# A two-layer hybrid decoder trunk: the memory's norm factors behind the memory rows, the first weight block in two halves, the sine's steps one block later

## What is computed

```python
def rms_norm(x, g):
    xf = x.astype(F32)
    y = xf * lax.rsqrt(jnp.mean(xf * xf, axis=-1, keepdims=True) + EPS)
    return (y * g.astype(F32)).astype(x.dtype)
...
    inv = 1.0 / (ROPE_BASE ** jnp.linspace(0.0, 1.0, half, dtype=F32))
    ang = positions.astype(F32)[..., None] * inv
    cos = jnp.cos(ang)[:, :, None, :]
    sin = jnp.sin(ang)[:, :, None, :]
...
    for l in range(DEPTH):
        g = norm_g[l]
        h = rms_norm(x, g[0])
        z = h @ w_in[l]
        ...
        x = x + rms_norm(mix @ w_out[l], g[1])
        mem_n = rms_norm(mem, g[6])
        x = x + rms_norm(memory_attention(rms_norm(x, g[2]), mem_n, x_wq[l], x_wkv[l], x_wo[l]), g[3])
        h = rms_norm(x, g[4])
        f = jnp.square(jax.nn.relu(h @ w_up[l])) @ w_down[l]
        x = x + rms_norm(f, g[5])
    return x
```

## Time and profile before

| | |
|---|---|
| median of 3 runs | 1506.36 us (1506.22 to 1506.47) |
| the profiled execution | 1506.58 us, of which the profile's span is 1504.5 us |
| PE busy | 1483.1 us, 99% of the span |
| DVE busy | 882.4 us, 59% |
| ACT busy | 634.4 us, 42% |
| POOL busy | 380.3 us, 25% |
| DMA | 162.09 MB, mean 108 GB/s; 288 GB/s in the first fortieth of the span |
| the chain that ended last | PE 94%, DVE 2%, DMA 1%, ACT 1%, issue 1% |

### The profile page before, as it was taken

The page is one execution under the profiler, slowest core; times in us unless marked ns, Lnnn a source line. Parts: engine busy times, 40 slices in busy tenths (PEclk is TensorE's granted clock), DMA queues, the critical chain, the costliest instruction groups (busy, mean ns, idle before and its releaser), DMA issues.

```text
span 1504.5 us, 19092 instructions
## 1 busy us (share of the span) xinstructions
PE 1483.1 (99%) x7842; PEld 1267.1 (84%) x7842; DVE 882.4 (59%) x1010; ACT 634.4 (42%) x883; POOL 380.3 (25%) x272
## 2 busy tenths in 40 slices
PE   8999999999999999999999999999999999999997
PEld 7878898888898888888898888988888988888886
DVE  5345556724367666575982465756245585756658
ACT  6335424524344343443562454335344352434344
POOL 2001720300053422315030028102001715151422
PEclk9999999999999999999999999999999999999999
DMA  8333131431223424152343232135203342433402
GB/s 288 90 98 101 53 112 65 150 122 54 94 106 115 137 85 162 62 168 99 112 133 119 64 95 86 67 105 175 84 29 112 112 147 79 141 110 112 140 28 98
DMA packets 83237, 162.09 MB, mean 108 GB/s; under 512 B 3664, under 2 KB 19792, under 8 KB 83152
## 3 DMA queue, kind: packets, MB, share of 16 engines
q1 hardware_dynamic: 81712, 158.35, 31.5%
q10 hardware_dynamic: 1440, 2.53, 0.5%
HBM read 158.78 MB, written 2.10 MB: 107 GB/s over the span
## 4 chain that ended last, share of the span: by engine, by line
PE 94%; DVE 2%; DMA 1%; ACT 1%; issue 1%; POOL 0%; SPq 0%; POOLq 0%; DVEq 0%; ACTq 0%
PE proj L688 26%; PE proj L690 25%; PE proj L689 25%; PE work L888 2%; PE work L690 2%; PE work L688 2%; PE work L689 2%; PE work L717 2%; PE work L867 2%; PE work L753 1%; DMA w_raw<-in_x_wkv_dram 1%; PE work L764 1%; PE work L743 1%; PE work L842 1%; PE work L821 0%
## 5 line engine op out<-in xcount | busy, mean ns | idle before, releaser
L1379 DVE TENSOR_TENSOR w_lo<-w_raw,w_hi 128x2048 fp32r<-128x2048 f32 (+1 forms) x103 | 234.8, 2280 | 274.9 <-ACT w_hi L1078 274.6
L688 PE MATMUL proj<-hT_hi,w_hi 128*128 128x512 f32 (+1 forms) x800 | 298.5, 373 | 0.0
L689 PE MATMUL proj<-hT_lo,w_hi 128*128 128x512 f32 (+1 forms) x800 | 297.7, 372 | 0.0
L690 PE MATMUL proj<-hT_hi,w_lo 128*128 128x512 f32 (+1 forms) x800 | 297.7, 372 | 0.0
L1078 ACT ACTIVATE w_hi<-w_raw 128x2048 fp32r<-128x2048 f32 (+1 forms) x103 | 185.3, 1799 | 234.2 <-PE proj L690 232.2
L688 PE MATMUL proj<-w_hi,hT_hi 128*128 128x512 f32 (+1 forms) x640 | 238.5, 373 | 3.5 <-ACT kmT L1182 2.2
L690 PE MATMUL proj<-w_hi,hT_lo 128*128 128x512 f32 (+1 forms) x640 | 232.3, 363 | 0.0
L689 PE MATMUL proj<-w_lo,hT_hi 128*128 128x512 f32 (+1 forms) x640 | 231.8, 362 | 0.0
L690 PEld LDWEIGHTS proj<-hT_hi,w_lo 128*128 128x128 f32 x800 | 150.7, 188 | 26.3
L689 PEld LDWEIGHTS proj<-hT_lo,w_hi 128*128 128x128 f32 x800 | 150.7, 188 | 26.1
L688 PEld LDWEIGHTS proj<-hT_hi,w_hi 128*128 128x128 f32 x800 | 150.7, 188 | 26.0
(11 more groups left out here) (197 smaller groups left out, 2446.3 us busy)
## 6 DMA issues: line engine op xcount, KB each, us to landing
w_raw<-in_w_up_dram SPq DMA_DIRECT2D x32, 1024.0 KB, 5.7
w_more<-in_w_down_dram SPq DMA_DIRECT2D x24, 1024.0 KB, 5.1
w_raw<-in_w_in_dram SPq DMA_DIRECT2D x28, 768.0 KB, 4.4
w_raw<-in_x_wkv_dram SPq DMA_DIRECT2D x15, 1024.0 KB, 5.1
w_raw<-in_w_out_dram SPq DMA_DIRECT2D x8, 1024.0 KB, 5.0
w_raw<-in_x_wq_dram SPq DMA_DIRECT2D x8, 1024.0 KB, 5.1
w_raw<-in_x_wo_dram SPq DMA_DIRECT2D x8, 1024.0 KB, 5.1
w_hs<-in_w_down_dram SPq DMA_DIRECT2D x8, 1024.0 KB, 5.1
```

The lines of the kernel that those rows point to most:

```text
L688: nc.tensor.matmul(dst, l_hi, r_hi, start=first, stop=False, skip_group_check=more)
L689: nc.tensor.matmul(dst, l_hi, r_lo, start=False, stop=False, skip_group_check=more)
L690: return nc.tensor.matmul(dst, l_lo, r_hi, start=False, stop=last, skip_group_check=more)
L1379: nc.vector.tensor_tensor(w_lo[:, slot, :, 0:cols], w_raw[:, raw, :, 0:cols], w_hi[:, slot, :, 0:cols].bitcast(F32), ALU.subtract).then_in ...
```

## The change

The memory's norm factors are issued by SP behind the two memory tiles, and no longer by ACT ahead of everything. ACT and DVE serve the first memory tile's turned rows ahead of block 0's first half, and the second tile's ahead of the second half. PE has a function of its own for block 0 (`first_block`): for all four tiles it multiplies the first half (two of the four 128-row parts), then for all four the second. The first half waits for three of the four turned lo parts and for a new semaphore on the first half's w_lo. DVE makes w_lo of block 1 ahead of the angle's steps. ACT's sin, cos and Exp-table steps move from ahead of the loop into block 1, behind w_hi of block 2.

```diff
             for t in range(MT):
                 sp.dma_start(mems[:, t], mem[0, t * P:(t + 1) * P]).then_inc(mem_first[t], 16)
+            load_gain(0, "mem")
             for h in range(2):
...
+            def first_block():
+
+                for h in range(2):
+                    if h:
+                        pe.wait_ge(w_lo_done, nth(w_lo_done, 0, 1))
+                    else:
+                        pe.wait_ge(turned_lo, nth(turned_lo, 0, -1))
+                        pe.wait_ge(w_first_lo, 1)
+                    for t in range(4):
+                        r = slice(t * P, (t + 1) * P)
+                        if h == 0:
+                            pe.wait_ge(added, nth(added, 0, t + 1 - T))
+                        for k in (2 * h, 2 * h + 1):
+                            mm = three_passes(proj[:, t, 0:MEM], w_hi[:, 0, k, r], w_lo[:, 0, k, r],
+                                              memT_hi[:, k], memT_lo[:, k], k == 0, False)
+                        if h:
+                            mm.then_inc(tile_done, 1)
+                pe.wait_ge(turned_lo, nth(turned_lo, 0, 0))
...
-                    if name == "km0":
+                    if name == "km0" and l == 0:
+                        first_block()
+                    elif name == "km0":
...
             start_counts(act, emptied, p_copied, c_copied, x_exped, x_copied)
-            act.dma_start(gains[:, GAIN_SLOT["mem"]], norm_g[0:1, GAIN["mem"]].broadcast_to([P, D])).then_inc(gain_loaded["mem"], 16)
             act.dma_start(ident[:], c_ident).then_inc(ident_loaded, 16)
...
-            for t in range(MT):
-                turn_hi(PROLOGUE, ("memk", t), memT_hi, t)
+
+            turn_hi(PROLOGUE, ("memk", 0), memT_hi, 0)
+            first_hi(0)
+            turn_hi(PROLOGUE, ("memk", 1), memT_hi, 1)
+            first_hi(1)
             split_hi(PROLOGUE, BLOCKS + 1)
...
-            act.wait_ge(trig_done, 1)
-            nc.scalar.activation(sin[:], angle[:], ACT.Sin)
-            nc.scalar.activation(cos[:], turns[:], ACT.Sin).then_inc(trig_done, 1)
-            nc.scalar.activation(table[:], minus_half[:, 0:1], ACT.Exp)
+
+            def turn_positions():
+                act.wait_ge(trig_done, 1)
+                nc.scalar.activation(sin[:], angle[:], ACT.Sin)
+                nc.scalar.activation(cos[:], turns[:], ACT.Sin).then_inc(trig_done, 1)
+                nc.scalar.activation(table[:], minus_half[:, 0:1], ACT.Exp)
...
                     if 0 < b < HEAD_BLOCKS - 1:
                         head_split(l, b + 1)
+                    if (l, b) == (0, 1):
+                        turn_positions()
                     before_block(l, b)
...
-            for t in range(MT):
-                turn_lo(PROLOGUE, ("memk", t), memT_hi, memT_lo, t)
+            turn_lo(PROLOGUE, ("memk", 0), memT_hi, memT_lo, 0)
+            first_lo(0)
+            turn_lo(PROLOGUE, ("memk", 1), memT_hi, memT_lo, 1)
+            first_lo(1)
+            split_lo(PROLOGUE, BLOCKS + 1)
             setup_steps = [0]
...
             dve.sem_inc(trig_done, 1)
-
-            split_lo(PROLOGUE, BLOCKS + 1)
```

More of the change, by code:

```diff
@@ L438, in trunk @@
         w_first_hi = ctx.enter_context(nc.semaphore("w_first_hi"))
+        w_first_lo = ctx.enter_context(nc.semaphore("w_first_lo"))
         const_loaded = ctx.enter_context(nc.semaphore("const_loaded"))
@@ L1031, in _ @@
                         b = FIRST_BLOCK[name] + kb
+                        if l == 0 and b == 0:
+                            continue
                         if t < tiles:
@@ L1327, in _, with first_hi @@
                 nc.scalar.activation(squares[:, t], mems[:, t], ACT.Square, accum_out=mem_sumsq[:, t:t + 1]).then_inc(mem_summed, 1)
-            for h in range(2):
+            def first_hi(h):
                 k = slice(BK // 2 * h, BK // 2 * (h + 1))
@@ L1815, in _, with first_lo @@
                 norm_mem(PROLOGUE, "memk", t)
-            for h in range(2):
+            def first_lo(h):
                 k = slice(BK // 2 * h, BK // 2 * (h + 1))
@@ L1821, in _ @@
                     dve.wait_ge(w_first_hi, 1)
-                part_lo = nc.vector.tensor_tensor(w_lo[:, 0, k], w_raw[:, 0, k], w_hi[:, 0, k].bitcast(F32), ALU.subtract)
-                if h:
-                    part_lo.then_inc(w_lo_done, 1)
-            for t in range(MT):
-                turn_lo(PROLOGUE, ("memk", t), memT_hi, memT_lo, t)
+                nc.vector.tensor_tensor(w_lo[:, 0, k], w_raw[:, 0, k], w_hi[:, 0, k].bitcast(F32),
+                                        ALU.subtract).then_inc(w_lo_done if h else w_first_lo, 1)
+            turn_lo(PROLOGUE, ("memk", 0), memT_hi, memT_lo, 0)
[3 more added lines that the diff above has]
+            split_lo(PROLOGUE, BLOCKS + 1)
             setup_steps = [0]
```

## The result

| | before | changed |
|---|---|---|
| median | 1506.34 us (8 runs, 1506.16 to 1506.47) | 1511.26 us (8 runs, 1510.05 to 1512.02) |
| profiled execution | 1506.58 us | 1511.43 us |
| span | 1504.5 us | 1509.5 us |

The ratio is 1.0032, with a 95% interval of 1.0023 to 1.0040: 4.9 us slower, where 0.9 was forecast and 1509.2 was the upper end of the range.

A forecast was written before the change was run, and what follows sets the result against it. PE, busy 99% of the span, was taken as the bound, already waiting for block 2. The start's 2.2 us gain is eaten there, and the sine adds 0.9 to the median 1506.36: 1507.3, range 1506.0 to 1509.2.

The forecast's parts named there:

- The bound: Before block 2: PE, busy 99% of the span, already waits there, so gains in blocks 0 and 1 are lost.
- Part 4: Sine steps on ACT behind block 2's w_hi: PE starts block 2 at 29.2, not 28.28, 0.9 us later.
- Part 3: Block 2's load: issued some 1.6 us later, yet landing again at 23.98, so zero change.
- Rival A: PE's clock falls in the 3.7 us gap before block 2, costing 1.6 us more: 1508.9; chance 0.28.
- The sum's last step: Behind block 2's start: PE works without a gap, so the 0.9 us is carried to the end.
- Rival C: Before block 2: PE keeps the 2.2 us of its early start, giving 1504.2; chance 0.04.

The follow-up runs named there:

- a2: The kernel before with only ACT's sin, cos and Exp-table steps moved behind block 2's w_hi: 1507.22 us, ratio 1.0006.
- c1: The kernel before with only block 2's load issued later, at 15.79 instead of 13.51: 1506.40 us, ratio 1.0000.
- b3: The changed kernel with five instead of three filling products ahead of block 0, which puts PE's start back: 1509.66 us, ratio 1.0023.
- d1: The changed kernel with block 2's load issued ahead of x tiles 2 and 3 and the sine's steps ahead of block 5: 1504.70 us, ratio 0.9988.
- a3: The changed kernel with the norm factors and the sine put back as in the kernel before: 1509.11 us, ratio 1.0019.
- a4: The changed kernel with only the sine's steps put back ahead of the loop: 1509.20 us, ratio 1.0020.

## Why the prediction was wrong

- **The bound was read rightly.** "Whatever blocks 0 and 1 gain is lost in front of" block 2: PE started block 0 1.85 us sooner, at 14.09 (forecast 2.2 and 13.7, at latest 14.0), and lost it all. The factors landed for the norm at 8.05, outside the 7.0 to 7.6 given. The second memory tile did come sooner, at 6.15 and not 7.58, but from 6 to 8 us the DMA engines moved 216 and 253 GB/s in the two microseconds and not 327 and 320; why is open.
- **Part 4, the sine, held** in place, releaser and size: 0.98 us from w_hi to PE's start in the changed kernel and in a2, where 0.9 was forecast.
- **Part 3, "I take zero", was the first term that failed.** Block 2's weights came 1.63 us later, outside the bounds of −1.0 to +0.5. The reason given there, that a later issue changes nothing in a full queue, was right (c1). What the step left out is that the landing follows PE's start (b3), through one late share of sixteen, most probably that of the DMA engine that fetches 16 KB of instructions. That packet stood in the trace of before, 1.6 us long, starting a microsecond before block 2 landed.
- **Rival A was the case that came**, and it had been given 0.28. The gap was 5.0 us instead of 3.7: 1.6 more by the later landing, 0.4 less since PE ended block 1 at 25.87 and not at 25.5. The price was 2.12 instead of 1.6. The step that failed is that the rivals were priced one by one from the forecast's gap; a later landing lengthens the gap, so the two belong together. With both, 0.98 + 1.63 + 2.12 = 4.73, which is what the profile shows. The range's upper end, 1509.2, had room for the sine and the landing (1509.0), not for the sine and the clock at its measured price (1509.4), and not for all three.
- **The sum's last step held**: of the 4.73 us none was given back behind block 4, and 0.12 came to it.
- **Rival C, "hardly possible"**, did not come; it had been tied to block 2's data by about 21. Once the load stood ahead of two x tiles, that data was there at 22.0 and four fifths of its 2.2 us were kept (d1).

## What to carry to other kernels

Before work is moved forward, look at what the waiting engine waits for next: here a load at the end of a full DMA queue took all of the gain, and its place in the queue was the edit that paid (0.74 us alone, 1.84 to 1.98 with the early start). A load has landed with its last share: when one comes late, look whether all of it was slow or one share. An idle stretch of TensorE can have two prices, its length and the clock behind it, and a term that lengthens the stretch can bring the second with it; price them together. Short work of no urgency, such as a table load, goes where its engine idles for long, not between two things that are waited for.

## What the runs showed of the hardware

- **The clock fell after 1.89 us of idleness** in b3 (and in eight of its ten runs), stayed after 1.37 us in a2 (in all ten) and after 3.09 us in the profiled run of a3. From block 2's start to block 4's a fall cost 1.2 us (a4: 17.71, not 16.48) to 2.1 us (the changed kernel: 18.60). The length of the last gap alone does not tell whether it comes.
- **A 16 KB packet of instruction fetches took 1.1 us (changed) to 1.6 us (before).** A 1 MB load at the 402 GB/s of the earlier trace rows takes 2.6 us (an estimate from that rate), so the packet is about half as long as a whole load.
- **One share of a load can come far behind the other fifteen.** In each of the fourteen profiles the load of block 2, of block 3 or of x tile 3 ends so, by 0.59 to 1.65 us, behind the first fetch. Why is not shown.
